# A hybrid decoder layer on one core: the expert stage with one-hot slot tables, three weight slots and sums kept in DRAM

## The reference, cut to what matters

```
n  = rms_norm(h, norm2_g)
lg = n @ wg + bg;  g = argmax(lg);  p_group = softmax(lg)[g]
le = (n @ we + be) restricted to group g's 4 experts
two best experts; weights p_group * softmax(two values)
for e in range(16):                     # gate, up: 1024x256, down: 256x1024
    he = silu(n @ w_gate[e]) * (n @ w_up[e])
    y += combine[:, e] * (he @ w_down[e])
out = (h + y)[16:]
```

## Time and profile before

| | us |
|---|---|
| timed runs | 1188.7, 1190.62, 1200.11 (median 1190.62) |
| profiled execution: span, first to last instruction | 1187.1 |
| its own device time | not listed by itself; the lowest timed run is 1.6 above the span |
| PE busy | 1036.4 (87%) |
| DVE, ACT, POOL busy | 318.4, 265.2, 65.4 |
| DMA over the span | 117.31 MB, mean 99 GB/s |
| last output product ends | 888.95 |
| expert 0's gate and up product begins | 929.26 |
| last down product ends | 1148.98 |

### The profile page before, as it was taken

One profiled execution on the slowest core, in us unless ns is written; L12 is line 12 of the kernel. 1 busy time (PEld: TensorE's weight loads), 2 busy tenths in 40 slices (PEclk: granted clock), 3 DMA queues, 4 the chain that ended last, 5 costly groups with the idle time before them and its releaser, 6 DMA issues.

```text
span 1187.1 us, 15771 instructions
## 1 busy us (share of the span) xinstructions
PE 1036.4 (87%) x6518; PEld 619.7 (52%) x6518; DVE 318.4 (27%) x691; ACT 265.2 (22%) x498; POOL 65.4 (6%) x186
## 2 busy tenths in 40 slices
PE   1998998998989678999999999999995899999950
PEld 1786776876667434555544444433455454444420
DVE  1113452223222237221123333344113411111103
ACT  4102521110211656223300000500132111111200
POOL 7600000000000000000000000000000100000001
PEclk9998899999999879999999999999995799999995
DMA  6122021104000200311111110421008388999946
GB/s 178 47 71 72 1 55 19 46 3 170 2 2 2 54 1 19 89 53 37 35 36 36 36 36 1 177 71 35 18 0 283 124 285 286 299 317 293 318 134 209
DMA packets 105255, 117.31 MB, mean 99 GB/s; under 512 B 15440, under 2 KB 92368, under 8 KB 105184
## 3 DMA queue, kind: packets, MB, share of 16 engines
q1 hardware_dynamic: 101728, 103.72, 28.0%
q0 software_dynamic: 3456, 12.58, 3.2%
HBM read 100.01 MB, written 16.25 MB: 98 GB/s over the span
## 4 chain that ended last, share of the span: by engine, by line
PE 73%; DMA 10%; DVE 5%; issue 5%; ACT 5%; SPq 1%; DVEq 0%; POOL 0%; ACTq 0%; POOLq 0%
PE ps L1297 14%; PE ps L1199 8%; DMA arena<-in_moe_w_up 7%; PE ps L1126 6%; PE ps L1145 6%; PE ps L1439 6%; PE ps L1465 5%; PE ps L1506 4%; PE ps L1150 4%; PE ps L1520 3%; DMA arena<-expert_rows,rows 2%; PE ps L1365 2%; ACT L480 1%; PE ps L1398 1%; PE ps L1399 1%
## 5 line engine op out<-in xcount | busy, mean ns | idle before, releaser
L1297 PE MATMUL ps<-arena 128*128 128x512 f32 x384 | 182.5, 616 | 1.0 <-ACT yT L583 0.3
L1506 PE MATMUL ps<-arena 128*128 128x512 f32 x256 | 119.3, 621 | 14.7 <-DMA arena<-in_moe_w_up 14.0
L1297 PEld LDWEIGHTS ps<-arena 128*128 128x128 f32 x384 | 70.7, 196 | 72.1 <-issue 70.7
L1199 PE MATMUL ps<-arena 64*64 64x64 f32 x2376 | 82.4, 223 | 12.5 <-DVE arena L808 10.8
L1199 PEld LDWEIGHTS ps<-arena 64*64 64x64 f32 x2376 | 75.3, 137 | 33.5 <-issue 25.5
L1506 PEld LDWEIGHTS ps<-arena 128*128 128x128 f32 x256 | 49.9, 198 | 81.9 <-issue 80.8
L1145 PE MATMUL ps<-arena 128*128 128x264 f32 x320 | 84.3, 407 | 0.2 <-ACT arena L517 0.2
L1126 PE MATMUL ps<-arena 128*128 128x264 f32 x320 | 72.5, 386 | 2.6 <-ACT arena L496 1.3
L454 POOL DMA_INDIRECT arena<-n_rows,idx x16 | 15.2, 948 | 1048.0 <-DVE idx L1012 1048.0
L1439 PE MATMUL ps<-yT,arena 128*128 128x512 f32 x144 | 68.0, 614 | 0.0
L1126 PEld LDWEIGHTS ps<-arena 128*128 128x128 f32 x320 | 60.0, 189 | 14.8 <-issue 2.8
(11 more groups left out here) (317 smaller groups left out, 1199.2 us busy)
## 6 DMA issues: line engine op xcount, KB each, us to landing
arena<-in_moe_w_gate SPq DMA_DIRECT2D x16, 1024.0 KB, 10.1
arena<-in_moe_w_up SPq DMA_DIRECT2D x16, 1024.0 KB, 12.6
arena<-in_moe_w_down SPq DMA_DIRECT2D x16, 1024.0 KB, 6.6
arena<-in_w_in SPq DMA_DIRECT2D x24, 512.0 KB, 3.9
arena<-in_w_in SPq DMA_DIRECT2D x9, 1024.0 KB, 5.4
expert_rows<-arena SPq DMA_DIRECT2D x16, 512.0 KB, 6.6
arena<-in_w_out SPq DMA_DIRECT2D x1, 4096.0 KB, 13.1
expert_rows<-h SPq DMA_DIRECT2D x7, 512.0 KB, 9.9
```

The costliest lines, as they stand in the source:

```text
L1199: ins = mm(psf[q, 512 * bank + c * CH:512 * bank + (c + 1) * CH], lhs(q, c), rhs(q, c), start=True, stop=True)
L1297: ins = mm(ps[:, 5 + 2 * (n % 2), :], gate_w[:, (n + 1) % 4, c, :], nT[:, c, META:L], start=(c == 0), stop=(c == DC - 1))
L1506: ins = mm(ps[:, bank, :], xgT[:, s, c, :], w1[:, s, c, :], start=(c == 0), stop=(c == DC - 1))
```

## The change

1. Router. PE transposes `h` itself, by halves, as soon as each half is added (`second_norm_T(t, part)`); ACT copies chunks 0 to 3 and DVE chunks 4 to 7. The gain is multiplied into the router weights at the start (`rw * g2c`), and the inverse root multiplies the finished logits. ACT alone computes the norm, with one table for `Ln` and `Exp`; `n2` no longer holds the gain. PE order: half 0 of t, transposes of t-1, half 1 of t, (for t = 3 its first transposes), logits of t-1.
2. Routing. `first` uses four operations; DVE needs 21 operations to `assign_ready`. Ranks and totals take 5 products (one of 64 columns, four with up to 64 columns). One table per choice, `slot_val` (token number and weight by expert) and `hit` (rank equals 0..127), and 8 products of 128x32 give, for all 16 experts at once, tokens, weights and destination rows (`slots`): `idx`, `coef`, `dest`. `index` leaves the loop.
3. Expert loop. Three slots for `w1`, `w2`, `xg`, `yo`. The copies of `rows_T` move from ACT to DVE, where they multiply by the gain. PE's order is as below. `yo` is scaled by `coef` while it is copied.
4. Sums. `h` is written to `y_dram` (512 rows and 128 spare ones for empty slots). POOL adds each expert's 128 rows to it by an indirect transfer with `compute_op=ALU.add`, each waiting for the one before. At the end SP copies `y_dram` to `out`, DRAM to DRAM.
5. Transfers. SP loads expert 0's gate and up after the last gate product; the rest of experts 0 to 2 when `merged` is ready, before and around the output product. The seven fills of `y_dram` and the broadcast of the gain go; one small parameter load comes.

```
-            for t in range(NE):  ...
+            sp.wait_ge(sem("gate_psum"), 3 * DC)
+            expert_in(0, 0)
+            sp.wait_ge(sem("merged_ready"), DC)
+            expert_out(0, 0); expert_in(1, 1); expert_out(1, 1); expert_in(2, 2)
...
+            for t in range(3, NE):
+                sp.wait_ge(sem("gu_psum"), t - 2)
+                expert_in(t, t % 3)
+                sp.wait_ge(sem("down_psum"), t - 2)
+                expert_out(t, t % 3)
...
+            for t in range(NT):
+                sp.dma_start(out[t * P:(t + 1) * P, :], y_dram[t * P:(t + 1) * P, :])
```

POOL after the change:

```
+            for t in range(3):
+                rows_in(t, t)
...
+            for t in range(NE):
+                if t + 3 < NE:
+                    pool.wait_ge(sem("xgT_psum"), 2 * t + 2)
+                    rows_in(t + 3, t % 3)
+                pool.wait_ge(sem("y_low"), t + 1)
+                pool.wait_ge(sem("y_high"), t + 1)
...
+                if t >= 1:
+                    pool.wait_ge(sem(f"y_out{(t - 1) % 3}"), 16 * ((t - 1) // 3 + 1))
+                rows_back(t, t % 3)
```

PE after the change, step t:

```
+                    hidden_T(t - 1, (t - 1) % 2)
+                    gate_up(t, t % 2, t % 3, 2 + 4 * (t % 2), 32 * (t // 3 + 1))
                     rows_T(t + 1, ...)
-                    index(t + 2)
                     down(t - 1, ...)
```

More of the change, by code:

```diff
@@ L367, in _, with expert_in @@
[L367 to L370, removed]
+            def expert_in(t, s):
+                sp.dma_start(w1[s][:, :, 0:DE], m_gate[t, :, :].rearrange("(c p) n -> p c n", p=P)).then_inc(sem(f"moe_w{s}"), 16)
+                sp.dma_start(w1[s][:, :, DE:], m_up[t, :, :].rearrange("(c p) n -> p c n", p=P)).then_inc(sem(f"moe_w{s}"), 16)
@@ new lines, in _ @@
+            sp.dma_start(y_dram[SEQ:, :], h[:, 0, :]).then_inc(sem("sum_set"), 16)
+            for t in range(NT):
+                sp.dma_start(y_dram[t * P:(t + 1) * P, :], h[:, t, :]).then_inc(sem("sum_set"), 16)
+            sp.wait_ge(sem("wo_psum"), 2 * NT)
+            expert_out(2, 2)
+            for t in range(3, NE):
[3 more added lines that the diff above has]
+                expert_out(t, t % 3)
@@ L685, in silu, with hidden_T @@
+            def hidden_T(t, s, slot_free):
+                act.wait_ge(sem("hT_psum"), t + 1)
+                if slot_free:
+                    act.wait_ge(sem("down_psum"), t - 1)
+                a.activation(hT[:, s, :, :].rearrange("p c n -> p (c n)"), ps[:, 3, 0:2 * P], ACT.Copy).then_inc(sem("hT_ready"), 1)
             def silu(t, s, bank, slot_free):
@@ L1488, in _ @@
-            ins.then_inc(sem("rank_psum"), 1)
-            def index(t):
-                for k in range(NT):
-                    ins = mm(ps[:, 7, 0:1], Pm[:, k, :], tokid[:, k:k + 1], start=(k == 0), stop=(k == NT - 1))
-                ins.then_inc(sem("idx_psum"), 1)
-            def rows_T(t, s, landed_):
-                pe.wait_ge(sem(f"xg_in{s}"), landed_)
+                ins = mm(ps[:, 3, (t + 1) * NE:(NT + 1) * NE].rearrange("p (t e) -> p t e", e=NE), ones[:],
+                         asg[:, t:t + 1, :].broadcast_to([P, NT - t, NE]), start=False, stop=(t == NT - 1), skip_group_check=True)
@@ new lines, in _, with rows_T @@
+            ins.then_inc(sem("rank_psum"), 1)
+            for j in range(2):
+                pe.wait_ge(sem("hit_ready"), j + 1)
+                if j == 0:
+                    pe.wait_ge(sem("slot_val_ready"), 1)
+                for t in range(NT):
+                    q = j * NT + t
+                    ins = mm(ps[:, 7, 0:2 * NE], hit[:, q, :], slot_val[:, q, :], start=(q == 0), stop=(q == 2 * NT - 1))
+            ins.then_inc(sem("slots_psum"), 1)
+            def rows_T(t, s, xs_, landed_):
+                pe.wait_ge(sem(f"xg_in{xs_}"), landed_)
```

523 lines of the change are left out of this document (262 added, 261 removed).

## The result

The changed kernel takes 1134.96 us in the median (1133.78 to 1142.08, four runs) against 1190.01 us beside it (four runs): a ratio of 0.954, 95% interval 0.949 to 0.959. The forecast was 1134. The profiled execution spans 1132.8 us, 54.3 less than before. One run further down, of e6, fell in the chip's slower state (1427.8 us at a mean granted clock of 0.72, the others 0.93 to 0.94): its median counts it, its ratio does not.

A forecast was written before the change was run, and what follows sets the result against it. PE and DMA were both near their limits, waiting on each other through late load issue, with routing and end uncovered. Savings 11 + 29 - 3 + 20 = 57 from 1190.6 gave 1134 us, own range 1119 to 1148 (wider: 1118 to 1165).

The forecast's parts named there:

- The sum, 57: Whole kernel: savings of 11 + 29 - 3 + 20 = 57 us, giving 1134 us.
- Part A: Router and routing, from the output product's end to expert 0's product: 11 us saved (7 to 13).
- 7 if PE's clock is low when the last logits run: Router: lower bound of the 11 us saving, 7 us, if PE's clock is low at the last logits.
- Part B, PE's pace of 11.57: Expert loop: 11.57 us of PE per expert instead of 12.36; 29 us saved if PE alone sets the pace.
- Part B, the excess of 3: Expert loop: 3 us over PE's pace, from twelve steps' DMA deficit less 11 us of slack (0 to 9).
- Part B, the rate: Expert loop: transfers at 356 GB/s; a step's traffic takes 11.8 us without the addition's read, 13.2 with it.
- The scatter's landing, 8 us: Expert loop: a scatter with addition lands in 8 us (upper bound 23), hidden below PE's step.
- Part C: From the last down product to the end: 38.1 us before, 18 after; 20 us saved (5 to 25).
- The DMA pace: Rival, expert loop: DMA sets the pace, 1160 us, chance 0.24; signs: PE waits for `in_moe_w_up`, share near 1 throughout.
- The end without gain: Rival, end: last scatter and copies cost 37 to 38 us as before; 1153 us, chance 0.10.
- The slower kernel: Rival, expert loop: the chain of scatters sets the pace, 1244 us at a landing of 17; chance 0.06.
- P: Expert loop: price of one scatter in the chain, landing plus 1 us; the span passes 1187 from 14.6 us.

The follow-up runs named there:

- e6: Kernel before with three slots for the expert weights and loads issued one step earlier, all else as before: 1180.32 us, ratio 0.990.
- e1: Changed kernel with two slots for the expert weights instead of three: 1173.16 us, ratio 0.9885 of before.
- e4: Changed kernel with one more unneeded load of 1 MB per expert from expert 3 on: 1164.70 us.
- e5: Changed kernel with four one-column products of 128x128 added to PE's steps 1 to 14: 1146.10 us.
- e2: Changed kernel with three slots, but all weight loads issued after the output product as in the kernel before: 1141.59 us.
- e8: Changed kernel with the 48 small DVE operations of the overflow tables spread over steps 1 to 8 of the loop: 1136.58 us.
- e3: Changed kernel with the addition taken out of the scatters, which write over the residual rows (sums left out): 1132.64 us.
- e9: Changed kernel with sums made in `out` itself, empty slots left out by the bounds check, final copies gone: 1132.15 us.
- e10: Changed kernel with sums in `out` (e9) and overflow tables spread over the loop (e8): 1123.71 us, ratio 0.947.
- e11: e9 with an expert's tokens spread over all 128 slots instead of lying in the first ones: 1123.14 us.
- e12: Changed kernel with sums in `out`, overflow tables and tokens spread, and gathers leaving out empty slots too: 1121.96 us, ratio 0.941 of before.

## Why the prediction was right, point by point

- **What bounds the kernel.** Right. The order of the loads was the fault (e1, e6), and DMA and PE are level behind it (e4, e5).
- **The sum, 57, measured 55.9, and the time.** The forecast's span was 1130.1 and the trace has 1132.8: the terms are 1.1 short, and the part ahead, taken as it is, is 1.6 longer. That the time is missed by 1 us only is luck in part: median and profiled span were 3.5 apart before, which was carried over, and are 2.2 apart now. The lower bound, 1119, does not follow from the parts' own bounds; they give some 1124.
- **Part A, 11 us, measured 10.2.** The walk was met almost step by step: product + 2.7 (2.6 forecast), selection 5.1 (4.9), ranks 2.3 (2.2), tables 3.4 (3.3), slot products 3.6 (3.8), POOL's start and gather 5.3 (5.3). The bound "7 if PE's clock is low when the last logits run" was no risk: the clock was 1.00 there. One thing was missing: the early loads keep the writes of `n2` and the first gather out of the queue, 8.4 us (e2). The sum was right only because it took the gather at 4.43, the row without weights beside it, without saying that this row now needs the early loads.
- **Part B, PE's pace of 11.57.** It is 11.41. From expert 0's product to expert 15's the forecast had 178.4 us with its excess, and the trace has 177.1, with errors both ways: the first step was 12.7, not 13.4, and the second 12.9, not 11.57, since expert 1's product took 8.50 and not 7.03, begun after 3.26 us of standing for DVE (granted clock 0.83). I had named DVE's 48 operations as the cause of the pause, which e8 shows, but had let PE run at full pace straight after it.
- **Part B, the excess of 3.** It is 3.2, in seven steps that are 0.5 too long, and that it fits is luck in good part. For 3 the forecast needs 1.2 us of deficit in each of twelve steps less 11 of slack. The trace has about 0.5 to 0.7 per step (the waiting half's 11.9, and 4.19 MB at the first half's 347 GB/s, 12.1, against 11.41), and the lead is gone by expert 9, after some 5 us by the same estimate: a deficit taken too large and a slack taken too large cancel. The mechanism, transfers that are level with PE and use up the lead, is right. SP's issues stand 7 us while the weights land just in time, where I had expected them to land well before their use.
- **Part B, the rate.** The pace of the transfers is 11.9 us per step, next to the 11.8 that I had for the traffic without the read of the addition and far from the 13.2 with it. The rate of the waiting half, 350 GB/s over the 4.19 MB of a step, gives the same 12.0. It is also close to the 358 of the Trainium skill ("DMA: Bandwidth & Descriptors", section "Where 436 GB/s comes from"); but with the read counted against it that figure asked for an excess of 9, and the trace shows 3.2. Nor does it hold as a ceiling here: e3 moves 368 GB/s from 963.9 to 1089.5 with no pause, while e9 has pauses at 329. "The most that mixed traffic showed", 356, was too low as well: the kernel before has a stretch (985 to 993) at 366. And the 418 at 914 is not of down weights alone: expert 1's were issued at 903.65 and landed within 12.0 us, while the writes of `n2`, issued by 909.4, took up to 11.6. What an addition costs is 1.3 us of packet time, of which 0.5 us or little more shows in the pace; bytes per second do not tell it.
- **The scatter's landing, 8 us.** 9.2 in the loop (bounds 5 to 23), 6.1 at the end (6 taken). The chain of scatters never set the pace: POOL waited for a landing once, at the last (5.5 us in all).
- **Part C, 20 us, measured 18.5.** Of the miss, 1.0 is the last scatter's wait, 2.8 us and not 1.8, and 0.5 the copies, 10.0 and not 9.5.
- **Rivals.** The DMA pace was the nearest. Its mechanism is real at the boundary; e4, with 1 MB more per step, comes near what that kernel would have been (loop + 29.7, where the rival had + 26). One of its two signs, a share near 1 throughout, came in the changed kernel too (1.06 in both halves) and tells nothing. The end without gain is ruled out by the 20.2 us. The slower kernel would have needed P = 14.6; P was 9.2 + 1.6 of issue at most.

## What to carry to other kernels

When loads and products are nearly equal, first ask how many steps before its use a load is issued; a third slot moved a loop from 13.7 us per step to PE's own 12.3 with nothing else changed. Without it the rest of the change made the loop slower than before (226.7 us against 219.1). To see whether a queue is falling behind, look at how long SP stands in an issue. With three slots it was mostly 7 us and more in the kernels that came to pause (the changed one, e9, e10) and 0.6 to 2.4 in those that did not (e3, e5, e6, e11, e12), while the mean share of the engines was near or above 1 in all of them. And where a scatter leaves rows out, try to spread the rows that remain over the partitions: here it was worth 4 us in the loop and 2.4 at the end (e9 to e11).

## What the runs showed of the hardware that I had not expected

- An addition by the indirect transfer costs POOL more as well: 1.55 to 1.63 us for each instruction against 0.96 to 1.00 for a plain scatter and, in the median, 0.95 to 0.98 for a gather (e3 and the changed kernel).
- Halving a scatter's rows by the bounds check freed nothing while the rows lay together (down weights landed in 13.8 us), and freed the queue when they, and the reads of row 0 with them, were spread (5.3 us).
- A pause costs a step more than its own length. After 0.3 us the product takes 7.12 in the chain instead of 6.88, at a granted clock of 1.00; the timeline has 7.12 against 7.05, so most of the difference is overlap with the transposes before it that is gone; after 3.3 us in e1 it takes 8.80, and there the granted clock is 0.81.
- Four DRAM to DRAM copies of 0.5 MB took 10.0 us together, 211 GB/s.
- The part ahead of the change moves by up to 9 us between executions of nearly the same code (output product at 830 to 839), more than most of the effects studied here.
